# A transformer block on one core: front weight loads wait for the last product's own signal, grouped queries turned a step earlier, a branch product ahead of the last values

## The reference, cut to what matters

```
y = sigmoid(gate0)*(a @ w_branch[0]) + sigmoid(gate1)*(b @ w_branch[1]) + sigmoid(gate2)*(c @ w_branch[2])
x = x + mod[2] * (y @ w_out)
f = modulate(rmsnorm(x))
for e in range(16):
    y += combine[:, e] * ((silu(f @ w_gate[e]) * (f @ w_up[e])) @ w_down[e])
x = x + mod[5] * y
out = rmsnorm(x)
```

## Time and profile before

| | before |
|---|---|
| median of 3 runs | 721.85 us |
| profiled execution, its own time | 723.5 us |
| its span, first to last instruction | 721.6 us |
| TensorE busy | 696.8 us, 97% |
| VectorE busy | 288.9 us, 40% |
| ScalarE busy | 114.5 us, 16% |
| GpSimd busy | 179.5 us, 25% |
| read from HBM | 178.14 MB |
| mean granted TensorE clock | 0.99 |

### The profile page before, as it was taken

The page is one execution under the profiler, slowest core; times in us unless marked ns, Lnnn a source line. Parts: engine busy times, 40 slices in busy tenths (PEclk is TensorE's granted clock), DMA queues, the critical chain, the costliest instruction groups (busy, mean ns, idle before and its releaser), DMA issues.

```text
span 721.6 us, 8021 instructions
## 1 busy us (share of the span) xinstructions
PE 696.8 (97%) x3274; PEld 416.5 (58%) x3274; DVE 288.9 (40%) x505; ACT 114.5 (16%) x199; POOL 179.5 (25%) x128
## 2 busy tenths in 40 slices
PE   9999999999999999998999999998999999999994
PEld 5444586555775457777777878647444434434431
DVE  3339392677210475743343233325323113202315
ACT  4021011111000422221121240013000000000004
POOL 0008998799079000800000000000000000000013
PEclk9999999999999999999999999998999999999997
DMA  9994526762432332433471235997799999999992
GB/s 357 418 379 181 211 108 234 291 219 71 175 134 100 116 118 69 165 116 117 175 288 54 79 121 191 421 404 310 283 417 423 419 423 421 420 421 421 420 408 85
DMA packets 29509, 183.70 MB, mean 255 GB/s; under 512 B 3543, under 2 KB 5975, under 8 KB 14624
## 3 DMA queue, kind: packets, MB, share of 16 engines
q1 hardware_dynamic: 27600, 178.98, 62.5%
q0 software_dynamic: 1584, 3.97, 1.4%
q10 hardware_dynamic: 288, 0.23, 0.1%
HBM read 178.14 MB, written 6.82 MB: 256 GB/s over the span
## 4 chain that ended last, share of the span: by engine, by line
PE 90%; DMA 3%; DVE 2%; issue 1%; POOL 1%; ACT 1%; DVEq 0%; SPq 0%; POOLq 0%; ACTq 0%
PE bank L1180 20%; PE bank L797 18%; PE bank L801 10%; PE bank L793 8%; PE bank L814 6%; PE bank L1140 4%; PE bank L1019 4%; PE bank L820 4%; PE bank L944 2%; PE bank L965 2%; PE bank L846 2%; PE bank L952 2%; PE bank L807 2%; DMA y_rows<-sb,token_rows 1%; DMA sb<-y_rows 1%
## 5 line engine op out<-in xcount | busy, mean ns | idle before, releaser
L1180 PE MATMUL bank<-sb 128*64 128x512 f32 x768 | 166.8, 594 | 0.7 <-ACT sb L728 0.7
L797 PE MATMUL bank<-sb 128*128 128x256 f32 x576 | 128.5, 382 | 0.6 <-PE bank L793 0.3
L797 PEld LDWEIGHTS bank<-sb 128*128 128x128 f32 x576 | 108.3, 190 | 17.6 <-issue 3.8
L1180 PEld LDWEIGHTS bank<-sb 128*64 128x64 f32 x768 | 53.9, 137 | 106.9 <-issue 105.0
L583 POOL DMA_INDIRECT y_rows<-sb,token_rows x7 | 7.0, 1000 | 373.0 <-DVE sb L1737 373.0
L543 POOL TENSOR_TENSOR sb<-sb 128x1024 f32<-128x1024 f32 x32 | 67.4, 2108 | 58.7 <-DMA sb<-ada_w 36.4
L1369 DVE COPY sb<-bank 128x512 f32<-128x512 f32 x45 | 29.2, 685 | 104.6 <-PE bank L952 66.1
L801 PE MATMUL bank<-sb 128*128 128x512 f32 x160 | 70.2, 594 | 0.3 <-PE bank L797 0.3
L793 PE MATMUL bank<-sb 128*128 128x512 f32 x128 | 55.8, 593 | 0.3 <-PE bank L1019 0.3
L801 PEld LDWEIGHTS bank<-sb 128*128 128x128 f32 x160 | 29.9, 191 | 35.2 <-issue 35.2
L1702 DVE TENSOR_TENSOR sb<-sb,bank 128x512 f32<-128x512 f32 x8 | 5.5, 687 | 97.1 <-PE bank L1180 97.1
(11 more groups left out here) (246 smaller groups left out, 674.3 us busy)
## 6 DMA issues: line engine op xcount, KB each, us to landing
sb<-expert_w SPq DMA_DIRECT2D x90, 1024.0 KB, 19.4
sb<-front_w SPq DMA_DIRECT2D x19, 2048.0 KB, 8.2
sb<-ada_w SPq DMA_DIRECT2D x32, 512.0 KB, 3.3
sb<-ada_mix SPq DMA_DIRECT2D x4, 2048.0 KB, 19.6
sb<-expert_w SPq DMA_DIRECT2D x12, 512.0 KB, 11.0
sb<-xcT SPq DMA_DIRECT2D x4, 512.0 KB, 6.3
sb<-front_w SPq DMA_DIRECT2D x4, 512.0 KB, 20.3
y_rows<-sb SPq DMA_DIRECT2D x4, 512.0 KB, 23.8
```

The source lines that it names most:

```text
L797: ins = pe.matmul(ps[:, c * L:(c + 1) * L], lhs(w, k, (2 * i + c) * P), hT[:, k, 0:L], start=(k == 0), stop=(k == KD - 1))
L1180: ins = pe.matmul(bank[e * CAP:(e + 1) * CAP, :], lhsT[:, k, e * CAP:(e + 1) * CAP], weights_at(k, e), start=(k == 0), stop=(k == parts - 1))
```

## The change

Three things change.

1. `w_used` goes. TensorE no longer waits or raises it after the last fill of a group; SP waits for `fill_ready` to reach the count of the group's last fill (`multiplied`).
2. The grouped queries are transposed in step 7, behind `values(6)` and ahead of that step's filler; the keys behind the filler and ahead of `turn_probs(7)`. In step 7, VectorE copies the three out behind its normalising and ahead of the probabilities. The wait for the third copy stays at the head of step 8. `SHARED` has the three entries ahead of the probabilities of step 7.
3. The first of the four fills of br0 is made ahead of `values(15)`.

```diff
+def multiplied(name):
+
+    return max(n for n, f in enumerate(FILLS) if f[0] == name) + 1
...
+GQA_TURN = 2 * 4 - 1
...
 for _i in range(STEPS):
-    if _i == 2 * 4:
+    SHARED += [("ada", g) for g in ada_in_step(_i)]
+    if _i == GQA_TURN:
         SHARED += [("gqT", 0), ("gqT", 1), ("gkT", 0)]
-    SHARED += [("ada", g) for g in ada_in_step(_i)]
     SHARED += [("pT", 2 * _i), ("pT", 2 * _i + 1)]
...
                 if earlier(n):
-                    sp.wait_ge(w_used, taken(earlier(n)[-1]))
+                    sp.wait_ge(fill_ready, multiplied(FRONT[earlier(n)[-1]]))
...
                 ins.then_inc(fill_ready, 1)
-                if name not in [f[0] for f in FILLS[n + 1:]]:
-                    pe.wait_ge(fill_ready, n + 1)
-                    pe.sem_inc(w_used, 1)
...
-            pe.wait_ge(fill_ready, 4)
-            pe.sem_inc(w_used, 1)
             pe.wait_ge(small_in, 16)
...
             for i in range(STEPS):
                 if i == 2 * 4:
-                    turn_gqa()
                     pe.wait_ge(shared_out, shared_no("gkT") + 1)
                 scores(i)
                 for g in ada_in_step(i):
                     ada_turn(g)
                 if i:
                     values(i - 1)
+                if i == GQA_TURN:
+                    turn_gqa_queries()
                 for n in FILLER_AT[i]:
                     fill(n)
+                if i == GQA_TURN:
+                    turn_gqa_keys()
                 turn_probs(i)
+            pe.wait_ge(pv_out, 2)
+            fill(fill_no("br0", 0))
             values(STEPS - 1)
             for b in range(3):
-                if b == 0:
-                    pe.wait_ge(pv_out, 2)
-                elif b == 1:
+                if b == 1:
                     pe.wait_ge(b_ready, 1)
-                else:
+                elif b == 2:
                     pe.wait_ge(pv_out, 4)
-                for i in range(4):
+                for i in range(b == 0, 4):
                     fill(fill_no(f"br{b}", i))
...
-                if i == 2 * 4:
-                    for q in range(2):
-                        shared_copy(shared_no("gqT", q), gqT[:, 2 * q:2 * q + 2, :].rearrange("p a b -> p (a b)"))
-                    shared_copy(shared_no("gkT"), gkT)
                 maxima(i)
                 normalise(i)
                 for g in ada_in_step(i):
                     add_ada(g)
+                if i == GQA_TURN:
+                    for q in range(2):
+                        shared_copy(shared_no("gqT", q), gqT[:, 2 * q:2 * q + 2, :].rearrange("p a b -> p (a b)"))
+                    shared_copy(shared_no("gkT"), gkT)
```

More of the change, by code:

```diff
@@ L58 @@
 MIX_K = KD // MIXES
-def taken(n):
-    return n + 1
 def earlier(n):
@@ L303, in build @@
         pass_in = [[sem(f"pass_in{m}{e}") for e in range(2)] for m in range(3)]
-        w_used = sem("weights_used")
         ada_in, ada_part_used, ada_summed = [sem("ada_in0"), sem("ada_in1")], sem("ada_part_used"), sem("ada_summed")
@@ L461, in _ @@
             load_unit(3)
-            sp.wait_ge(w_used, taken(FRONT.index("gate5")))
+            sp.wait_ge(fill_ready, multiplied("gate5"))
             load_both(2)
@@ L467, in _ @@
             load_unit(9)
-            sp.wait_ge(w_used, taken(FRONT.index("br2")))
+            sp.wait_ge(fill_ready, multiplied("br2"))
             load_both(5)
@@ L472, in _ @@
             load_both(7)
-            sp.wait_ge(w_used, taken(FRONT.index("out0")))
+            sp.wait_ge(fill_ready, multiplied("out0"))
             load_both(8)
-            sp.wait_ge(w_used, taken(FRONT.index("out1")))
+            sp.wait_ge(fill_ready, multiplied("out1"))
             load_both(9)
@@ L909, in square_sums, with turn_gqa_queries @@
                               start=True, stop=True).then_inc(shared_ready, 1)
-            def turn_gqa():
+            def turn_gqa_queries():
                 pe.wait_ge(gqa_ready, 1)
@@ L919, in turn_gqa, with turn_gqa_keys @@
                     ins.then_inc(shared_ready, 1)
+            def turn_gqa_keys():
                 ps = take_shared(shared_no("gkT"))
```

## The result

| | before | after |
|---|---|---|
| median | 722.11 us (4 runs, 721.7 to 723.26) | 709.57 us (4 runs, 708.08 to 710.35) |
| ratio | | 0.9817, 95% interval 0.9803 to 0.9831 |
| profiled execution | 723.5 us, span 721.6 | 710.35 us, span 708.4 |
| TensorE busy | 696.8 us, 97% | 693.4 us, 98% |
| gaps of 0.30 us on TensorE that its own matmul ended | 20, behind every group but br2 | none |

What follows compares the result with a forecast made beforehand. TensorE's own queue, 90% of the chain, was taken as the bound, so every gap counts in full. Gains 9.2 + 1.4 + 1.1 = 11.7 us, from the runs' median 721.85 to 710.1 us; range 707.3 to 713.6.

Steps and rivals of the forecast that it cites:

- The counter: At TensorE's group ends: dropping the raising and 21 waits gains 9.2 us, bounds 5.7 and 9.9; nineteen at 0.47 each.
- The wait behind br2: Only the router's small product stands behind it; removing the wait gains 0.3 us, bounds 0 and 0.47.
- The last one: Wait behind out1: removal gains nothing, as the transposes after it need VectorE's residual anyway.
- The first rival: Each removed wait returns only its visible 0.30 us gap: 5.7 us from nineteen waits, 8.2 total, 713.6 us; 7%.
- The Trainium skill's 175 ns: Time for a matmul through the array; by it nineteen waits give 3.3 us, total 5.8, 716.0 us; within a 7% rival.
- Queries and keys: Seam of steps 7 and 8: block costing 3.4 us costs 2.0 in its new place, gain 1.4, bounds 0.9 and 1.9.
- The new short wait: Second half of step 7's probabilities waits for the keys' bank until VectorE has copied them; priced 0.5 us.
- br0: Before step 15's values: one 3.5 us fill covers the wait for VectorE's copies, gain 1.1 us, bounds 0 and 1.1.
- The experts' stream: Expert weight loads move with TensorE, some 3.5 us in hand; rival that they hold the end: 718.3 us, 4%.
- The clock: Low clock at routing costs the first gather 2.7 us; change counted as nothing, 1.5 us allowed on both sides.
- The slower rival: Low clock stays through routing and first experts, 0.39 us lost per us; 35 us more gives 723.8 us; 2%.
- The sign at the end of the front: In the changed profile the first router product starts earlier by about 11.7 us.

Runs made afterwards that it cites:

- the second fill: Changed kernel with two branch fills ahead of the last values in place of one: median 709.81 us, ratio 0.9828.

## Why the prediction was right

- **What bounds the kernel: right.** TensorE's queue. The stretch from the first expert product on is 214.9 to 215.0 us in the before, the changed and the parts' profiles, so all that the front gave came through.
- **The counter: right, a little small.** The step said 0.47 per wait, 8.9 + 0.3; the counter alone measured 0.485 per wait in the front and 9.7 us in all. The seams by themselves are 0.47; the rest is that the product behind a wait is slower too, 0.02 to 0.08 us. The wait behind br2, taken at 0.3 without a seam to read it from, comes out near: the last four branch fills took 445.76 to 459.96, 14.20 us, and four without a wait 13.85 (38.10 us for the eleven from 410.94 to 449.04), so 0.35. The last one, counted as nothing, gave 0.07: from the last out fill to the transposes it is 482.28 to 490.89 before and 470.78 to 479.32 after, where VectorE's residual now ends a gap of 0.27. The price was right as the sum, and the prediction left open what it was made of: 0.30 for the wait and 0.19 for the raising behind it, neither of which would have given 0.47 alone. Whether the 0.19 is the raising or only an instruction of its own there stays open. The first rival took the visible gap of 0.30 to be the gain when the counter goes; it fell.
- **The Trainium skill's 175 ns** (TensorE: Matmul & The Clock Gate, "Single matmul latency") is near to the 0.22 us that a seam loses by the wait alone, and says nothing of the second half. By it nineteen waits were 3.3 us; the counter gave 9.7.
- **Queries and keys: right.** 1.4 forecast, 1.47 measured alone. The new short wait was forecast at 0.5 and is 0.44; the queries cost 0.93 for 1.0. One sentence of the prediction is wrong: that all three copies are done before the filler ends. It holds for the queries' two (319.07 to 320.35, the keys follow the filler at 323.79). The keys' own copy starts at 324.42, and it is the wait that the same paragraph prices at 0.5.
- **br0: right.** 1.1 forecast, 1.10 measured alone, and the second fill shows that the cover is complete.
- **The experts' stream: right.** It moved with TensorE; 3.7 us are in hand, where the prediction read some 3.5.
- **The clock: counted as nothing.** In the two profiles the start lost 1.2 us and the routing gained 1.8 beside out0's wait, net 0.6, which the allowance of 1.5 us covered. In the medians the whole gained 12.5 us, and 13.2 when it ran again; 11.6 to 11.8 of that is in the front and 0.9 in ff's and out0's waits, which leaves 0 to 0.6 for the clock. That a loss at the start and a gain in the routing partly cancelled is luck. The slower rival, a low clock that stays, did not come: it lasted as long as before. The sign at the end of the front, the router's product earlier by 11.7, came as 10.92 (459.96 to 449.04), because the start had lost 1.2.

Not settled: what decides on which instructions the low clock falls. In these profiles it fell on the gather, on the products ahead of the wait, twice in the routing, or not at all there (counter only), with the same instructions there but for the number of warming products.

## What to carry to other kernels

A queue that waits for its own last result only to pass a signal on pays twice, for the wait and for the signal behind it; let the reader wait for the result's own signal. Compare starts to starts at seams with and without the thing, since the printed gap (0.30) was not the cost (0.47), and with the wait alone a cost of 0.30 had no printed gap at all. When parts of a change are timed alone, split the time by stretches: a stretch that jumps by itself, like the routing here, is counted into each part and makes the sum too large.

## What the runs showed of the hardware

- A wait of TensorE for its own last matmul cost 0.30 us here; a raising instruction behind it 0.19 more; that instruction without a wait nothing that the front shows (it is 0.4 us shorter).
- The next product's weight load, which ran 0.42 us ahead of its product, came only after the awaited product had ended: idle for 0.89 us in place of 0.24, and for 1.10 with the raising.
- In a wait behind every fill, 50 waits cost 14.76 us in the front: 0.295 each, the price that 18 waits showed.
- The granted clock fell to the low level behind 20-column products and transposes with hardly any idle time between them (478.1 to 482 in the changed kernel, with one gap of 0.27 us). In the kernel before it fell behind such products and 1.85 us of idle time, which I had put it down to; in the changed kernel it fell without it.
